# Rounding and subtracting the weights of a split-precision matmul kernel two chunks at a time

## The reference

```python
def even_layer(h, ...):
    p = rms_norm(h, norm_g) @ w_in            # 256 x 2048 @ 2048 x 10256
    ...
    o_a = (rms_norm(o, dn_norm_g) * gate_a)   # gated delta rule, per-head beta and decay
    o_b = silu(layer_norm(conv(glu))) * silu(z_b)
    o_m = memory_attend(q_m, z_m, q_norm_m, mem_k, mem_v)
    return concatenate([o_a, o_b, o_m]) @ w_out
def stick_breaking_attention(q, k, v):        # per block of 128 queries
    log_keep = where(mask, log_sigmoid(-z), 0)
    rest = cumsum(log_keep, reverse) - log_keep
    weights = where(mask, exp(log_sigmoid(z) + rest), 0)
    out = weights @ v
```

## Time and profile before

| | |
|---|---|
| time, median of 3 runs (lowest, highest) | 1384.59 us (1384.58, 1385.32) |
| the profiled execution's own time | 1385.76 us |
| its span, first to last instruction | 1384.0 us |
| mean granted TensorE clock | 0.995 |
| TensorE, VectorE, ScalarE busy | 1363.7, 890.0, 753.1 us |
| HBM | 234.32 MB read, 172 GB/s over the span |

### The profile page before, as it was taken

How to read it: one execution, slowest core, us unless ns; L and a number is a source line. 1 busy time by engine, 2 the same in 40 slices (tenths; PEclk the granted TensorE clock), 3 DMA queues, 4 the chain that set the end, 5 groups by cost and what they waited for, 6 DMA issues and landing times.

```text
span 1384.0 us, 17368 instructions
## 1 busy us (share of the span) xinstructions
PE 1363.7 (99%) x6473; PEld 1131.6 (82%) x6473; DVE 890.0 (64%) x1327; ACT 753.1 (54%) x1163; POOL 113.1 (8%) x112
## 2 busy tenths in 40 slices
PE   8999999999999999899999999999999999999998
PEld 7788888887888878788888888888888888888887
DVE  5457688887787888665566545654645745556563
ACT  5545543556435564665445455856756757665341
POOL 2001201012210100000000120020020100000000
PEclk9999999999999999999999999999999999999999
DMA  9655545554554675365464655464564564653652
GB/s 291 204 170 167 168 145 179 160 160 152 148 192 136 207 244 181 103 219 162 136 199 151 215 167 193 135 206 151 182 198 149 176 189 141 197 168 122 196 184 76
DMA packets 134477, 239.27 MB, mean 173 GB/s; under 512 B 13904, under 2 KB 19961, under 8 KB 134393
## 3 DMA queue, kind: packets, MB, share of 16 engines
q1 hardware_dynamic: 131641, 233.42, 53.3%
q10 hardware_dynamic: 2752, 4.73, 1.0%
HBM read 234.32 MB, written 3.80 MB: 172 GB/s over the span
## 4 chain that ended last, share of the span: by engine, by line
PE 89%; DVE 5%; issue 3%; ACT 2%; DMA 1%; POOL 0%; SPq 0%; DVEq 0%; ACTq 0%; POOLq 0%
PE job L1608 26%; PE job L1610 26%; PE job L1609 26%; PE mixer L1647 3%; DVE wlo L1245 2%; PE mixer L1856 1%; PE mixer L1876 1%; PE mixer L1748 1%; DVE reg L1319 1%; DMA raw<-in_ev_w_in_dram 1%; DVE cvr L1469 1%; PE mixer L1894 1%; PE mixer L1762 1%; PE mixer L1907 0%; PE mixer L1729 0%
## 5 line engine op out<-in xcount | busy, mean ns | idle before, releaser
L1608 PE MATMUL job<-whi,xhi 128*128 128x512 f32 x1724 | 693.4, 402 | 0.0
L1245 DVE TENSOR_TENSOR wlo<-raw,whi 128x1024 fp32r<-128x1024 f32 x432 | 528.4, 1241 | 230.5 <-ACT whi L912 228.0
L1610 PE MATMUL job<-whi,xlo 128*128 128x512 f32 x1724 | 675.6, 392 | 0.0
L1609 PE MATMUL job<-wlo,xhi 128*128 128x512 f32 x1724 | 674.0, 391 | 0.0
L912 ACT ACTIVATE whi<-raw 128x1024 fp32r<-128x1024 f32 x432 | 445.9, 1056 | 143.5 <-PE job L1610 134.9
L1610 PEld LDWEIGHTS job<-whi,xlo 128*128 128x128 f32 x1724 | 325.0, 189 | 70.5
L1609 PEld LDWEIGHTS job<-wlo,xhi 128*128 128x128 f32 x1724 | 326.0, 189 | 63.1
L1608 PEld LDWEIGHTS job<-whi,xhi 128*128 128x128 f32 x1724 | 325.4, 189 | 62.0 <-DVE xlo L1272 0.2
L1469 DVE SCALAR_TENSOR_TENSOR cvr<-cvr,vt 128x255 f32<-128x255 f32 (+14 forms) x240 | 106.9, 501 | 0.0
L939 ACT ACTIVATE proj<-job,rstd 128x512 f32<-128x512 f32 x80 | 50.5, 686 | 51.5 <-PE job L1610 44.2
L1261 DVE TENSOR_TENSOR hid<-hid,job 128x512 f32<-128x512 f32 x48 | 30.7, 681 | 50.1 <-PE job L1610 50.1
(11 more groups left out here) (266 smaller groups left out, 897.4 us busy)
## 6 DMA issues: line engine op xcount, KB each, us to landing
raw<-in_od_w_in_dram SPq DMA_DIRECT2D x160, 512.0 KB, 4.5
raw<-in_ev_w_in_dram SPq DMA_DIRECT2D x144, 512.0 KB, 4.2
raw<-in_ev_w_out_dram SPq DMA_DIRECT2D x48, 512.0 KB, 4.5
raw<-in_od_w_out_dram SPq DMA_DIRECT2D x48, 512.0 KB, 4.5
raw<-in_w_mem_kv_dram SPq DMA_DIRECT2D x32, 512.0 KB, 4.5
reg<-in_mem_dram ACTq DMA_DIRECT2D x4, 512.0 KB, 7.1
hid<-in_x_dram ACTq DMA_DIRECT2D x4, 512.0 KB, 5.9
out_dram<-hid SPq DMA_DIRECT2D x4, 512.0 KB, 2.7
```

Source lines behind the costliest of these rows:

```text
L1245: vec.tensor_tensor(wlo[:, c % RING, :, :], raw[:, c % RAWS, :, :], whi[:, c % RING, :, :].bitcast(F32), ALU.subtract).then_inc(s_lo, 1)
L1608: mm(out_, xh, hi, start=first, stop=False)
L1609: mm(out_, xh, lo, start=False, stop=False)
L1610: return mm(out_, xl, hi, start=False, stop=last)
```

## The change

From chunk 8 on, an even chunk's `split` handles two chunks in one instruction of 2048 columns on ScalarE and one on VectorE; an odd chunk's does nothing. The pair waits for both loads and, for chunks c and c+1, for TensorE to have done chunk c-5. It signals both at once. The ring has six slots in place of seven. The small weights `bah` and `bal` get tiles of their own, with no wait for the ring, and their steps, placed by `RING + 1`, move one position forward.

```diff
-RAWS, RING, AHEAD = 6, 7, 4
+RAWS, RING, AHEAD = 6, 6, 4
+SINGLE = 8
...
+        bah = sb("bah", [128, 16, 16], F32R)
+        bal = sb("bal", [128, 16, 16], F32R)
...
             def split(c):                      # ScalarE
-                sc.wait_ge(s_raw[c % RAWS], 16 * (c // RAWS + 1))
+                if c >= SINGLE and c % 2:
+                    return
+                n = 2 if c >= SINGLE else 1
+                for q in range(c, c + n):
+                    sc.wait_ge(s_raw[q % RAWS], 16 * (q // RAWS + 1))
                 if c >= RING:
-                    sc.wait_ge(s_pe, c - RING + 1)
-                if c == 2 * RING - 1:
-                    sc.wait_ge(s_bap, 1)
-                act(whi[:, c % RING, :, :], raw[:, c % RAWS, :, :], ACT.Copy).then_inc(s_hi, 1)
+                    sc.wait_ge(s_pe, c + n - RING)
+                act(whi[:, c % RING:c % RING + n, :, :], raw[:, c % RAWS:c % RAWS + n, :, :], ACT.Copy).then_inc(s_hi, n)
...
             def do_baw(_):
                 sc.wait_ge(s_small, 48)
-                sc.wait_ge(s_pe, RING)
-                act(bah, wba, ACT.Copy).then_inc(s_wbh, 1)
+                act(bah[:, :, :], wba, ACT.Copy).then_inc(s_wbh, 1)
...
             def split(c):                      # VectorE
-                ve.wait_ge(s_hi, c + 1)
-                vec.tensor_tensor(wlo[:, c % RING, :, :], raw[:, c % RAWS, :, :], whi[:, c % RING, :, :].bitcast(F32),
-                                  ALU.subtract).then_inc(s_lo, 1)
+                if c >= SINGLE and c % 2:
+                    return
+                n = 2 if c >= SINGLE else 1
+                ve.wait_ge(s_hi, c + n)
+                vec.tensor_tensor(wlo[:, c % RING:c % RING + n, :, :], raw[:, c % RAWS:c % RAWS + n, :, :],
+                                  whi[:, c % RING:c % RING + n, :, :].bitcast(F32), ALU.subtract).then_inc(s_lo, n)
```

More of the change, by code:

```diff
@@ L419, in prog @@
         bar = reg[0:2 * H_DN, 256:512]
-        bah = whi[:, RING - 1, 0, 0:256].rearrange("p (k n) -> p k n", k=16)
-        bal = wlo[:, RING - 1, 0, 0:256].rearrange("p (k n) -> p k n", k=16)
         def psum(name):
@@ L1280, in do_baw @@
                 ve.wait_ge(s_wbh, 1)
-                vec.tensor_tensor(bal, wba, bah.bitcast(F32), ALU.subtract).then_inc(s_wbl, 1)
+                vec.tensor_tensor(bal[:, :, :], wba, bah[:, :, :].bitcast(F32), ALU.subtract).then_inc(s_wbl, 1)
             def do_bat(_):
```

## The result

The changed kernel takes 1543.84 us (median of 4 runs, 1535.57 to 1547.7) against 1384.95 us: ratio 1.1139, 95% interval 1.1091 to 1.1187. It is 159 us slower where I had forecast 80, beyond the top of my range (1498). The profiled execution is the fastest of the four, with a span of 1533.8 us, 149.8 more than before.

The account below looks back on a forecast made before the run. TensorE, busy for 99% of the span, was taken as the only bound. Terms 29+16+11+7.5+6+12+14-2 = 93, less 13 for overlapping waits, gave +80 us on the 1384.0 us span: 1466 us as time, range 1428 to 1498.

Parts of the forecast that it names:

- term 7: Whole kernel: clock drops after five waits over 1.9 us and a third of the heads' waits, 7 us each.
- term 4: Start: the small product and chunk 8 come late behind the first pairs, 5.9 us, 7.5 with a clock drop.
- Term 1: 16 stick-breaking heads: the mask runs behind the pair's subtraction, making each value product 1.8 us late, 29 us.
- Term 2: Gate tiles: at ten even positions VectorE reads the bank late, delaying TensorE's next turn 1.6 us, 16 us.
- Term 3: LayerNorm stage: last tap with POOL's adds, squares' chain and square root run late behind pairs, 11 us.
- term 6: Smaller delays by the same rule: inverse's stores and updates, decays, a memory-fill bank, LayerNorm outputs, 12 us.
- Term 5: Delta rule, two groups: the factors start late behind the pair's subtraction, 3.3 and 2.5 us, sum 6 us.
- Gains: ScalarE and VectorE: 19 and 40 us of saved busy time bring nothing; freed transposes about 2 us.
- Neighbouring waits overlap ... I take off 13: Sum of terms: a wait lets VectorE catch up for the next, so 13 us are deducted.
- Rival C: Heads and gates: clock drops with every wait, +15 to +25 us more, or late loads; 1500 and more; chance 0.07.
- Rival B: ScalarE and VectorE: idle time absorbs longer instructions; start and longest cases remain, 1410 us (1390 to 1434); chance 0.13.
- Rival D: Weight preparation: copies' throughput caused TensorE's waits, so the change is faster, 1367 us; chance 0.02.

Follow-up runs that it names:

- Experiment 1: Changed kernel with every chunk split singly, keeping the ring of six and the moved small weights: 1386.78 us, ratio 1.0022 to the kernel before.
- Experiment 7: Changed kernel with seven more matmuls of 128 columns before each head's value product: 1532.49 us, ratio 1.1065 to the kernel before.
- experiments 9 to 11: Changed kernel with the pair on ScalarE alone, 1454.27 us; the kernel before with AHEAD = 3, 1391.17 us, and with AHEAD = 5, 1383.08 us.
- experiment 6: Changed kernel with each pair made by two 1024-column instructions on each engine, same place and wait: 1458.33 us, ratio 1.0528 to the kernel before.

## Why the prediction was wrong

The direction and the mechanism held. What failed were a deduction for overlap, a term for the clock that was far too small, and a kind of step put at nothing. The forecast of 80 us was some 65 of waits (the terms without the clock, less 13) and 15.6 of clock (term 7's 14, and the 1.6 in term 4). Measured in the profiled execution were 105.5 of waits and 44.3 of busy time. The waits, term by term, as growth of TensorE's own:

- Term 1, heads: 29 us forecast, 29.5 measured, with the copy, subtraction, mask and product in the order and at the distances worked out.
- Term 2, gates: 16 forecast, 20.0 measured (21.9 in eleven waits, less 1.9 that was there before).
- Term 3, LayerNorm: 11 forecast, 13.2 measured: 3.8 for POOL's sum and 13.4 in three waits for fills behind the chain, less 4.1 that was there. TensorE's idle time in that stage grew by 16.8 us (20.87 - 4.05); the other 3.7 are the weights themselves, which term 6 had at 3. The squares' chain started at T+4.5 to the hundredth. Timeline of VectorE in the changed kernel, T being 611.37:

```profile
613.66 2.29 DVE L1250 TENSOR_TENSOR wlo<-raw,whi 128x2048 fp32r<-128x2048 f32 x1 [3.08 <-ACT whi L915]
615.87 0.42 DVE L1487 COPY scr<-cvr 128x512 f32<-128x512 f32 x1
```

- Term 4, start: 5.9 of waits and 1.6 of clock forecast, 5.5 and 1.6 measured up to chunk 12; the small product starts at 45.31, forecast 45.1. Experiment 1, without pairs, has 1.9 of the 5.5 already, 1.4 of them before the small product (2.1 in place of 0.6): that part is the ring or the move, the rest the pair.
- Term 5, factors: 3.3 + 2.5 forecast. The two waits of L1652 for `cvr` L1086 are 7.9 us in total, 2.1 of which was there before: 5.8.
- Term 6, smaller ones: 12 forecast, some 17.5 measured, 5.0 of them before the inverse's matmuls (L1753), 3.7 for the weights, the rest in waits of 1.4 us at most.
- Gains: of the 2 us from transposes that would be freed nothing is seen. The saved busy time, 31.6 us on ScalarE and 29.5 on VectorE, is 0.15 and 0.14 us a pair, not 0.09 and 0.19: by busy time a single split had cost 1.03 and 1.22 us. The time doesn't depend on it.
- Left out: the fills of mixer outputs (`xlo` L1277) and of the hidden state, in stages where I had only looked for the gates. They stand behind the pair like all others: 9.9 + 3.3 us in six waits. Timeline of the changed kernel, VectorE and TensorE:

```profile
782.58 2.29 DVE L1250 TENSOR_TENSOR wlo<-raw,whi 128x2048 fp32r<-128x2048 f32 x1 [2.12 <-ACT whi L915]
784.78 0.75 DVE L1277 TENSOR_TENSOR xlo<-mix,xhi 128x256 fp32r<-128x256 f32 x2
...
785.59 0.71 PE L1613 MATMUL job<-whi,xhi 128*128 128x512 f32 x1 [2.08 <-DVE xlo L1277]
```

- "The weights themselves are in time, with 6 us to spare" failed in one place, the LayerNorm outputs. There ScalarE and VectorE hand each other 0.4 us steps, and with the pairs among them both fell behind: the pair 176, 177, which stands at position 172, was subtracted when TensorE had already finished chunk 175 and waited for it. VectorE, then TensorE:

```profile
669.34 2.29 DVE L1250 TENSOR_TENSOR wlo<-raw,whi 128x2048 fp32r<-128x2048 f32 x1 [0.99 <-ACT whi L915]
...
671.78 0.47 PE L1613 MATMUL job<-whi,xhi 128*128 128x512 f32 x1 [2.72 <-DVE wlo L1250]
```

Three things make up the miss of 40 us in the waits, a third each: the terms that I had were too low together (78 after the gains, some 92 measured), the fills were put at nothing (13.2), and 13 were deducted.

- **The step that failed in the waits: "Neighbouring waits overlap ... I take off 13".** Nothing was given back. Neighbouring gates, two positions apart, wait in full one after the other, and all 16 heads wait 1.8 to 1.9 us:

```profile
478.73 0.41 PE L1652 MATMUL mixer<-ident,proj 128*128 128x128 f32 x2 [1.89 <-DVE mix L1514]
488.29 0.41 PE L1652 MATMUL mixer<-ident,proj 128*128 128x128 f32 x2 [1.87 <-DVE mix L1514]
```

  My reading, argued and not tested by itself: a wait of TensorE also puts off chunk c-5, hence the next release, so the engines can't use it to catch up; ScalarE idled 462.3 us for that release.
- **The step that failed by the largest sum: term 7, the clock, with too few waits counted.** It had to carry the busy time, which grew by 44.3 us where I had 15.6 with term 4's part. By the mean granted clock, 0.029 x 1533.8 - 0.005 x 1384.0 = 37.6 of it is the clock; what the other 6.7 are stays open. I had taken some ten waits, at 1.4 us each. In windows of 4 us behind every wait of TensorE, 24 show a clock under 1.00, where the kernel before has four, and each lost 1.6 us on average: seven of the 16 heads, five of the eleven gates, four of the six fills left out, four in the LayerNorm stage, two at the start, one at the factors and one at the inverse. Experiment 7 prices the heads' part at 11 us by taking it away; the others weren't taken away.

The last 8 us, from this execution to the median of four, are clock too: the shortest and longest of the four have spans of 1533.8 and 1546.0 us at clocks of 0.971 and 0.963; the time lost to the clock is 44.5 and 57.2 us, a difference of 12.7 where the spans differ by 12.2. My forecast was made for one execution. The changed kernel spreads by 12 us over four; the kernel before by 1 over its four, and by 5.7 over the 17 timed beside experiments 9 to 11.

Rival C, the clock falling with every wait of terms 1 and 2, had 0.07. Its time (1500 and more) came true, its condition in part: 12 of those 27 waits. The forecast's waits and more drops of the clock came together, and the two belonged in one case. Of my signs of being wrong none came: the copies set out at T+0.28 in the head shown, the pairs took 1.92 and 2.31 us on average, and TensorE waited for no raw load. (ScalarE did, for 23.7 us in place of 7.8, and no wait of TensorE names it.) Rival B (absorbed) is excluded by the heads alone. Rival D and the saved busy time were rightly taken at nothing: 61 us fewer on two engines bought no time in any experiment. The Trainium skill (Perfetto Trace Analysis, Optimizing Scalar/DVE Operations) advises breaking instructions up where the engine isn't saturated and makes others wait; the 85 us between the changed kernel and experiment 6 agree with it.

## What to carry to other kernels

Work in engines that issue in order is priced by what is queued behind it at the moment it can start, not by its busy time: merging two instructions makes both the release later and the hold longer, and here the two together cost more than their sum (3, 24, 44 and 159 us). Merged early, they still cost 24 us and more: an early release is no early start. Look at each step that stands behind the merged one, in all stages, and don't discount their waits against each other where the release is given by the waiting engine itself. In this trace none of TensorE's 29 waits up to 1.8 us was followed by a clock under 1.00, and 24 of the 36 longer ones were: count the clock for waits of such a length, and expect the runs to spread.

## What the runs showed of the hardware

After waits of 1.86 and 1.87 us of the same form the granted clock was 1.00 once and 0.57 once. A longer wait doesn't settle it either: two of 3.47 us, ending at 166.44 and 424.52 us of the changed kernel, were followed by 1.00 and 0.65:

```profile
166.44:170.44 4.00, 4.00 (x20) 3.30 (x21) 0.00 (x0) 1.09 (x2) 4.00 (x13) 1.00 0.57 214
424.52:428.52 4.00, 4.00 (x16) 3.59 (x17) 1.34 (x2) 2.40 (x2) 0.00 (x0) 0.65 1.04 392
```

Its four executions had mean clocks of 0.963 to 0.971 and spans 12 us apart. Seven matmuls of 128 columns in each of 16 waits, 112 more matmuls (224 more instructions in the trace), made the kernel 11 us faster.
